# A hybrid decoder block on one core: last product by token halves, first V blocks loaded beside the stream, two more lead tiles, no row reads due ahead of an output product, ranks moved

## The reference, cut to what matters

```python
a = rms_norm(h, g_mix)                       # 1024 tokens, D = 1024
q, k, v, g_ret, cb, cc, ch, gate_r, gate_c = split(a @ w_in)
ret = silu(g_ret) * head_group_norm(chunkwise_retention(rotary(q), rotary(k), v))   # 4 heads
z = causal_short_conv(cc * ch)
merged = sigmoid(gate_r) * (ret @ w_ret_up) + sigmoid(gate_c) * ((cb * z) @ w_conv_up)
h = h + merged @ w_out
# PEER: 8 heads pick 16 of 128*128 experts each, per token
xb = rms_norm(h, g_ffn);  idx, score = product_key_top16(xb @ w_peer_q)
act = gelu(einsum('td,ted->te', xb, u[idx]))
h = h + einsum('te,ted->td', softmax(score) * act, v[idx])
h = h + sigmoid(rms_norm(h, g_ple) @ w_ple_gate) * (p @ w_ple_proj)
out = rms_norm(h, g_final)
```

## Time and profile before

| | |
|---|---|
| median of 3 runs | 3687.8 us (3678.93 to 3694.53) |
| the profiled execution's own time | 3681.89 us |
| its span | 3680.1 us |
| TensorE matmul / weight load busy | 3420.2 us (93%) / 3353.9 us (91%) |
| VectorE, GpSimd, ScalarE busy | 2709.3, 2170.0, 1195.2 us |
| mean granted TensorE clock | 0.966 of full |
| HBM traffic | 231 GB/s over the span |

### The profile page before, as it was taken

One profiled execution on the slowest core, in us unless ns is written; L12 is line 12 of the kernel. 1 busy time (PEld: TensorE's weight loads), 2 busy tenths in 40 slices (PEclk: granted clock), 3 DMA queues, 4 the chain that ended last, 5 costly groups with the idle time before them and its releaser, 6 DMA issues. The chain is left out here.

```text
span 3680.1 us, 59182 instructions
## 1 busy us (share of the span) xinstructions
PE 3420.2 (93%) x22379; PEld 3353.9 (91%) x22379; DVE 2709.3 (74%) x4191; ACT 1195.2 (32%) x1855; POOL 2170.0 (59%) x1406
## 2 busy tenths in 40 slices
PE   7899978989999889899999999998999999989987
PEld 6799978989999789899999999997999999989965
DVE  5524368676886666998989898652888888888854
ACT  2310131232221233455656555542222222222232
POOL 5478755323687555566666666664666666656521
PEclk9999989999999899999999999998999999999998
DMA  4233322112688768788888888897988989979701
GB/s 150 81 114 122 130 97 69 61 48 74 230 312 304 257 217 280 250 314 291 314 293 307 305 307 308 320 345 248 316 307 304 315 314 317 323 267 325 244 18 63
DMA packets 324155, 851.86 MB, mean 231 GB/s; under 512 B 27536, under 2 KB 125328, under 8 KB 320656
## 3 DMA queue, kind: packets, MB, share of 16 engines
q0 software_dynamic: 110592, 402.70, 30.6%
q1 hardware_dynamic: 72864, 258.15, 20.5%
q10 hardware_dynamic: 140528, 188.78, 14.7%
HBM read 754.62 MB, written 94.90 MB: 231 GB/s over the span
## 5 line engine op out<-in xcount | busy, mean ns | idle before, releaser
L582 POOL TENSOR_TENSOR w_lo<-raw,w_hi 128x1024 fp32r<-128x1024 f32 x206 | 544.8, 2645 | 434.4 <-ACT w_hi L1017 430.6
L681 PE MATMUL main<-mix_hi,w_hi 128*128 128x320 f32 (+1 forms) x2816 | 689.9, 319 | 52.9 <-issue 17.1
L681 PE MATMUL main<-mix_lo,w_hi 128*128 128x320 f32 (+1 forms) x2816 | 677.2, 314 | 0.0
L681 PE MATMUL main<-mix_hi,w_lo 128*128 128x320 f32 (+1 forms) x2816 | 676.3, 314 | 0.0
L609 POOL DMA_INDIRECT rows<-v_rows,s_idx x384 | 391.4, 1019 | 335.2 <-DVE scr L1632 273.2
L681 PEld LDWEIGHTS main<-mix_hi,w_hi 128*128 128x128 f32 x2816 | 480.7, 191 | 57.8 <-issue 40.5
L1632 DVE SCALAR_TENSOR_TENSOR scr<-rows,s_dot,scr 128x1024 f32<-128x1024 f32 x381 | 487.9, 1281 | 45.1 <-DMA rows<-v_rows,s_idx 34.6
L926 PE MATMUL main<-h_hi,v_hi 128*128 128x320 f32 x2048 | 474.9, 313 | 38.0 <-DVE res L2022 20.8
L681 PE MATMUL main<-a_hi,w_hi 128*128 128x320 f32 (+1 forms) x1728 | 466.7, 324 | 34.4 <-POOL w_lo L582 18.2
L609 POOL DMA_INDIRECT rows<-u_rows,s_idx x384 | 390.2, 1016 | 162.3 <-DVE s_dot L1625 85.2
L681 PEld LDWEIGHTS main<-mix_lo,w_hi 128*128 128x128 f32 x2816 | 484.0, 191 | 0.0
(11 more groups left out here) (243 smaller groups left out, 5310.7 us busy)
## 6 DMA issues: line engine op xcount, KB each, us to landing
raw<-stream SPq DMA_DIRECT2D x474, 512.0 KB
act_d<-actb ACTq DMA_DIRECT2D x128, 320.0 KB
gate_d<-gbuf ACTq DMA_DIRECT2D x20, 2048.0 KB, 10.1
h<-act_d ACTq DMA_DIRECT2D x128, 320.0 KB
gate_in<-gate_d ACTq DMA_DIRECT2D x31, 1280.0 KB
rows<-u_rows,s_idx POOLq DMA_INDIRECT x384
rows<-v_rows,s_idx POOLq DMA_INDIRECT x384
score_d<-stage ACTq DMA_DIRECT2D x16, 320.0 KB
```

Of the source, the lines that this page charges most:

```text
L582: pool.tensor_tensor(w_lo[:, s, :], raw[:, s, :], w_hi[:, s, :].bitcast(F32), ALU.subtract) \
L681: last = pe.matmul(main[s][:, dst:dst + n], wt[:, s, c * P:(c + 1) * P], rows[:, c, src:src + n], start=(c == 0 and wt is w_hi and rows is ...
```

## The change

What it does, by place:

- `LEAD` is 6, not 4: six expert tiles run ahead of the first selection, and 12, not 14, behind the fifth block.
- `rate` gives 0 also to the two tiles ahead of the output product (78 and 79 of pass two), and 32 for 31 elsewhere in pass two. `due` of tiles 77, 79, 80 and 81 is now 115, 118, 118 and 121. The 506 stay 506.
- `add_out` waits for its own row of x, not for all eight.
- The first four V blocks are read into a place of their own (`v_raw`) by ScalarE's queue at expert tile 116, cast in tiles 121 to 124 and subtracted by GpSimd behind the splits of tiles 123 to 126. The first gates are read at tile 116 too, the first activations at tile 119, and the four casts `h_cast` come in tile 126. GpSimd's row reads of the V stage wait until the first gates are used up (`h32_ready`).
- The projection's halves have places of their own, `p_whi` and `p_wlo`; the first two F tiles are split without a wait for it. `ple_part(1)` comes behind the norm's mean.
- The last product runs as 16 tiles of 512 tokens (the eight weight tiles are loaded and split twice); the first half's norm, rows and stores lie beside the second half's tiles.
- 20 of the 44 rank parts go into the heads and the first step behind them.
- The copy of the third block of sparse tokens' inputs to PSUM (`swap_at`) comes one step earlier, at the last quarter of the first block.

The diff, cut to its core:

```diff
-LEAD = 4
+LEAD = 6
...
-    if tile < PICKED_AT or 2 * Q_PAIR - 2 <= tile < 2 * Q_PAIR:
+    if tile < PICKED_AT or 2 * O_PAIR - 2 <= tile < 2 * O_PAIR or 2 * Q_PAIR - 2 <= tile < 2 * Q_PAIR:
         return 0
     if tile < 2 * S1:
-        return 31
+        return 32
...
+                first = tile - (2 * B_PAIR - EG - 1)
+                if 0 <= first < EG:
+                    pool.wait_ge(v_hi_made, first + 1)
+                    pool.tensor_tensor(v_lo[0][:, first, :], v_raw[:, first, :], v_hi[0][:, first, :].bitcast(F32),
+                                       ALU.subtract).then_inc(v_split, 1)
...
             pool.wait_ge(tile_done, 2 * B_PAIR)
+            pool.wait_ge(h32_ready, EG)
...
+            pool.wait_ge(s_added, 1)
+            for t in range(2 * DC):
+                if t == 2:
+                    odd_rows(4, 8 * DC + 2, b_lo, b_hi, rowb[2])
+                pool.wait_ge(raw_in[t % 2], 16 * (F_PAIR - EG // 2 + t // 2) + 16)
+                if t >= 2:
+                    pool.wait_ge(tile_done, F_TILE + t - 1)
+                pool.tensor_copy(w_hi[:, t % 2, :], raw[:, t % 2, :]).then_inc(hi_made, 1)
...
             ple_part(0)
-            ple_part(1)
             pe.wait_ge(s_added, NS)
             norm_mean(4, 2, 0)
-            for n in range(2, DC):
+            for n in range(1, DC):
                 ple_part(n)
...
+            for t in range(2 * DC):
+                half, n = divmod(t, DC)
+                tile_mm(F_TILE + t, F_MAIN + t // 2, t % 2, b_hi, b_lo, norm=4 if t == 0 else None,
+                        parts=((0, half * HALF, HALF),))
+                if t == DC + 1:
+                    out_mean(0)
+            out_mean(1)
...
+                if e == LEAD + SPAN * (ND - 1) + QUARTERS[15] + 2:
...
+                    load_gates(0, gate_first)
+                    for k in range(EG):
+                        act.dma_start(v_raw[:, k, :], stream[2 * (B_PAIR - S1) + k]).then_inc(v_raw_in, 16)
-                if e == NE - 5:
+                if e == NE - 9:
                     act.wait_ge(dot_done, LAST_LOW + 1)
...
-                            rank_some((21 if first else 7, 8)[e])
+                            rank_some((21 if first else 9, 10)[e])
...
+                        dve.wait_ge(x_in[ps][2 * i + s], 32)
                         dve.wait_ge(tile_done, 2 * (base + O_PAIR + i) + s + 1)
...
-                for c in range(DC):
-                    dve.wait_ge(x_in[ps][c], 32)
...
-            rank_some(44)
+            rank_some(24)
...
+                if t == DC + 3:
+                    out_rstd(0)
+                if DC + 4 <= t < DC + 8:
+                    for c in range(2):
+                        out_row(0, 2 * (t - DC - 4) + c)
+            out_rstd(1)
```

More of the change, by code:

```diff
@@ L556, in _, with split @@
                     load(B_PAIR - S1 + i, s)
[L557 to L564 removed]
+            for t in range(2 * DC):
+                sp.wait_ge(tile_split, F_TILE + t - 1)
+                load(F_PAIR - S1 + t % DC // 2, t % 2)
+            for half in range(2):
+                at = slice(half * HALF, (half + 1) * HALF)
+                for c in range(DC):
+                    sp.wait_ge(out_ready, DC * half + c + 1)
+                    sp.dma_start(out_t[c * P:(c + 1) * P, at], res[:, c, at]).then_inc(out_st, 16)
+            sp.wait_ge(out_st, 16 * 2 * DC)
         @block.gpsimd
         def _(pool):
[L569 to L570 removed]
+            def split(pair, s, tile, peeled, past_v=False):
+                pool.wait_ge(raw_in[s], 16 * (pair - EG // 2 * past_v) + 16)
                 if not peeled:
@@ L972, in ple_part, with out_mean @@
                                              wt[:, n // 4, col:col + P], pt[:, c, half * HALF:(half + 1) * HALF],
-                                             start=(c == 0 and wt is w_hi and pt is p_hi),
-                                             stop=(c == 1 and wt is w_lo))
+                                             start=(c == 0 and wt is p_whi and pt is p_hi),
+                                             stop=(c == 1 and wt is p_wlo))
                 last.then_inc(tile_done if n % 4 == 3 else ple_filled, 1)
+            def out_mean(half):
+                pe.wait_ge(sq_added, DC * (6 + half))
+                at = half * HALF
+                pe.matmul(scr[half][:, 0:HALF], ones_d[:, :], nt2[2][:, at:at + HALF], start=True, stop=True) \
+                    .then_inc(stat_filled, 1)
             ple_part(0)
-            ple_part(1)
             pe.wait_ge(s_added, NS)
             norm_mean(4, 2, 0)
-            for n in range(2, DC):
+            for n in range(1, DC):
                 ple_part(n)
-            with pe.Fori(0, DC // 2) as i:
-                for s in range(2):
-                    tile_mm(F_TILE + 2 * i + s, F_MAIN + i, s, b_hi, b_lo, norm=4 if s == 0 else None)
-            norm_mean(5, 2, 0)
+            for t in range(2 * DC):
+                half, n = divmod(t, DC)
[4 more added lines that the diff above has]
+            out_mean(1)
         @block.scalar
@@ L1309, in h_cast @@
                 act.copy(h_hi[b % 2][:, k, :], h32[b % 2][:, k, :]).then_inc(hhi_ready, 1)
-            swap_at = min(m for m in range(16 * ND) if due(2 * S1 + tile_of(m) - 1) > 2 * P)
+            swap_at = min(m for m in range(16 * ND) if due(2 * S1 + (tile_of(m) if m % 16 < 15 else LEAD + SPAN * (m // 16 + 1)) - 1) > 2 * P)
             for e in range(NE):
@@ L1398, in _ @@
             ple_out(0)
-            ple_out(1)
             norm_std(4, 2, 0)
-            for n in range(2, 4):
+            for n in range(1, 6):
                 ple_out(n)
@@ L1868, in mixers @@
                 steps.then(dve.memset(nt2[ps][:, :], 0.0))
-                for c in range(DC):
-                    dve.wait_ge(x_in[ps][c], 32)
-                if ps == 0:
-                    with dve.Fori(0, DC // 2) as i:
-                        add_out(i)
-                else:
-                    for i in range(DC // 2):
-                        add_out(i)
+                for i in range(DC // 2):
+                    add_out(i)
                 norm = 1 + 2 * ps
```

141 lines of the change are left out of this document (78 added, 63 removed).

## The result

The changed kernel takes **3663.0 us** (median of four runs, 3661.33 to 3668.43) against 3689.2 for the kernel before in the same four rounds: a ratio of 0.9939, 95% interval 0.9925 to 0.9954. That is faster by 0.6% (the medians are 0.7% apart), but 26 us where 62 were forecast, and 7 us above the range. The profiled execution took 3661.97 us, its span is 3660.2.

What follows compares the result with a forecast made beforehand. The bound was TensorE's own work wherever it doesn't wait. Gains of 17 + 14 + 12 + 19 = 62 us off the profiled 3681.9 gave 3619.9; with the runs' median 5.9 higher, the forecast was 3626, range 3602 to 3656.

Steps and rivals of the forecast that it cites:

- Output product, 17: Output product of pass two: removing TensorE's 15.6 us wait for a low half and low-clock loss gains 17 us (13 to 19).
- Lead of six, 14: First selection: two more expert tiles fill TensorE's 16.5 us wait for picked_ready, gaining 14 us (8 to 16.5).
- Junction, 12: Expert stream to V blocks: the second V group starts at 2582 instead of 2594.2, gaining 12 us (3 to 20).
- V blocks, 0: The 31 later V groups: no instruction changed, periods stay at 29.54 us, costed at nothing.
- rival 4: V blocks: splits stand behind runs of eight row reads, period grows to 34.45, 3778 us; chance 0.05 in full or part.
- End, 19: Last product and the tail behind it: 19 us gained together (8 to 22).
- The tail's 8: Behind TensorE's last matmul: 1024-column operations are halved, 22.5 us shrink by 10.3, 3 given back: 8 us (2 to 11).
- The product's 11: Last product: last row 12.3 us earlier, then 15 half tiles; TensorE's last matmul near 3638.3 instead of 3649.2: 11 us.
- my low end: Last product: a gain of 6 us in place of 11 if ScalarE's copies of ple stay in the way.
- Rival 2: Last product and tail: GpSimd's 16 splits hold VectorE back, 8 us in place of 19, 3637 us; chance 0.13.
- The ports: Last product: by the skill's shared-port rule alone, first-half rows pile up behind the last matmul, time near Rival 2's.
- Ranks, 0 within 2: Heads: 20 rank parts of 0.7 us go where VectorE was idle: nothing, within 2 us either way.

## Why the prediction was wrong

- **Output product, 17:** right, 17.8 us. The wait for w_lo is gone, and x was there in time.
- **Lead of six, 14:** right where it was made (15.1), wrong as a sum. The two tiles moved TensorE's loop over the blocks by some 200 instructions, and three jumps took 12.6 us back; the written-out kernel with a lead of four shows the 12 us that the lead is worth without them. I had seen the 5.06, 4.98 and 4.10 us there, called issue, had taken them for a fixed cost that no edit of this change touches, and had put no row of them into the prediction. They were neither fixed nor untouched, and I had no rival for it.
- **Junction, 12:** half right. The second group came 8.1 us earlier; VectorE was stopped for 6.56 us by a cast behind a late V block, a wait that the new order made. What failed is the cost of the new reads themselves: ScalarE stands while it issues 2 MB of reads into a busy queue, and I had charged it nothing. It was 6.7 us, so the net is 1.4.
- **V blocks, 0:** right (0.4), and rival 4 didn't come.
- **End, 19:** 11.5. The tail's 8 was 11.0: the backlog that I had given back was smaller. The product's 11 was 0.5. Two steps failed. The input's last row came 8.8 us earlier (40.6 us behind the V blocks' last matmul for 49.4), not 12.3, since ScalarE's copies of ple stood ahead of its casts (VectorE waited 4.06 us for them); that was the condition of my low end. And I had counted 15 half tiles behind the last row where whole tiles leave only 14 halves' worth and a rest: the row-by-row wait is worth less matmul work when each row feeds half the columns, which cost 7 us with the clock; and I had put TensorE at full pace behind it, where the late sigmoid and the lower clock behind it took most of another 6. Rival 2 (8 for the end) was the nearest case, and for a part of its reason.
- **The ports.** The Trainium skill, page "SBUF — State Buffer", section "🔬 SBUF: two separate sides", says that of a VectorE operation with two SBUF inputs and a GpSimd operation the one that starts first holds the shared ports for the whole instruction. The trace agrees: an operation of VectorE that began 0.38 us behind a split of 2.72 us took 2.88 us for 0.69, and ended 0.54 us behind it. It hardly set TensorE's pace, though: in the stretch from 3557 us on, TensorE was busy for 80.3 of 83.2 us.
- **Ranks, 0 within 2:** wrong by 13.0 us, the largest miss. The row I read (VectorE idle for 4.13 us in the second head) shows idle time at one place, but the 20 parts were put at others, behind the norm and ahead of the states, on the chain that sets the head's end; 6.2 us of TensorE's wait for exactly that signal were in the trace, and I hadn't looked at it.
- **The range** added up the low ends of the terms I had and held nothing for terms at zero. The heads, the jumps and the issue of the reads, 32 of the 42 us that were missing, were steps costed at nothing.

## What to carry to other kernels

A hole that the profile calls issue, at a place where a loop of an engine jumps back, is a cost that can be removed by writing the loop out, and that can grow when an edit ahead of it moves the code; look for such holes first, since here they were worth as much as all the order of the work. An engine's idle time is slack only if the signal it sends next isn't waited for: ask who waits for the next signal behind the place where work is put. And where a tile is fed row by row, halving its width halves the work that hides the feeding.

## What the runs showed of the hardware

- A jump back of TensorE's loop of some 1300 matmuls cost about 7 us (21.6 us for three in the kernel before: 14.1 us of holes, the rest mostly the lower clock behind them), and 10 in the mean where a second hole followed 6 matmuls later (30.6 us for three, of which 24.4 holes); 18 more instructions ahead of the loop took the second hole away (one execution).
- Four reads of 512 KB issued by ScalarE in one piece held it for 10.96 us; one of them right behind another read 6.17 us, one alone 0.37.
- The granted clock was 0.63 over 23 us in which TensorE did 42 matmuls in small pieces, and 1.00 over 16 us with as many matmuls (busy 10.9 us) in the kernel with whole tiles.
- An operation of VectorE with two inputs of 512 columns took 0.69 us alone and 2.88 behind a split of 2.72 us that had just begun on GpSimd.
